# A hybrid decoder block: the next block's x rounded in one run, v ahead of the scores, one masked operand per subtile

## The chip, the cores and the metric

The kernel runs on one core of a Trainium2 chip. The metric is the device time of one execution in microseconds (us). A core has TensorE (PE, matrix products), VectorE (DVE), ScalarE (ACT), GpSimd (POOL) and SyncE (SP, which here only issues DMA transfers). PE writes its results to PSUM, eight banks of 2 KB for each of 128 partitions, and DVE and ACT read them there. Every engine runs its own stream of instructions in order and waits on semaphores.

## What is computed

One layer over 4096 tokens of width 1024: a normalised input, one input projection, three mixers (pooling, convolution, attention in a sliding window), a gate on each, one output projection and a last normalisation. The change touches the attention and what feeds it:

```python
h = rms_norm(x, ln_g[l])
proj = jnp.einsum('bsd,de->bse', h, w_in[l])
(u_pool, g_pool, c_a, c_b, g_conv, q, k, v, g_attn) = split_columns(proj)
...
# attention: 8 query heads on 2 key heads of 64, window of 128 tokens
qb = q.reshape(B, nb, BLOCK, N_KV_HEADS, Q_PER_KV, HEAD_DIM) * (HEAD_DIM ** -0.5)
kb = jnp.concatenate([kr[:, :-1], kr[:, 1:]], axis=2)   # the tile before, and the own
scores = jnp.where(valid, scores + bias, -1e30)         # ALiBi; 0 <= distance < 128
p = jax.nn.softmax(jnp.concatenate([scores, sink], axis=-1), axis=-1)[..., :-1]
out = jnp.einsum('bnkgqs,bnskd->bnqkgd', p.astype(v.dtype), vb)
...
x = x + jnp.einsum('bse,ed->bsd', y, w_out[l])
return rms_norm(x, final_g)
```

## The kernel before

The program has two stages. The attention stage goes through eight blocks of 512 tokens (`NB`), each of four subtiles of 128 (`SUB`). The mixer and output stage behind it starts with `cb0` at line 346's products and is not touched.

Projections are made in fp32 accuracy from three products: weights and x are each split into a rounded part (`hi`, by ACT) and a remainder (`lo`, by DVE), and hi·hi, lo·hi and hi·lo are added up. A tile of the projection (`project`) is 8 slices of x (`kk`) by 3 matmuls of 128x512, so 24. A block has ten tiles in this order: k, q0 to q3, v, g0 to g3. The q tiles fill the four `wide` banks, which later hold the scores; the others take the two `pair` banks in turn. `K_LAG` lets the products with the remainder run three slices behind in k.

x of the next block (n+1) is prepared in block n: loaded into `xs` (two DMAs on SP, two on ACT, `load`), squared and summed (`square` on ACT, lines 239; `square_more` on DVE, line 248), folded on PE (`fold_sums`, line 276, in q3, into bank `turn0`), made a mean (`mean`, DVE, line 282) and a root (`root`, POOL), scaled (`scale`, ACT, line 294, four parts), turned in squares of 32 (`turn_squares`, DVE, line 301), and split (`split_hi`, ACT, line 333; `split_lo`, DVE, line 339) into `xT`, where it overwrites the slices of block n: `spent` says that g3 has used them. `store_xT` sends `xT` to HBM in two pieces of 2 MB for the later stage.

The attention of a subtile j: `scores` on PE (lines 1280, 1289) into `wide`; `take_scores` on DVE in two halves of four heads (mask by `copy_predicated`, line 1037; bias and row maximum, line 1041; then line 1046 and 1047); `exps` on ACT (lines 902, 905); `invert` on DVE; `normalise` on POOL (line 845); `turn_squares_of_probs` on DVE (line 1066), which turns squares of 32 inside the tile `rows`; `store_probs` and `load_probs` on SP, which go through HBM (`p_scratch`) so that the squares come back in transposed places, into `whole`; and `mask` on POOL (lines 855, 856). The window needs two operands: where a query's 64 tokens ("early" or "late" half) see only a part of a key tile, keys of one half belong to the tile before and keys of the other to the own tile. `mask` writes the part for one tile into `rest` (times `rest_mask`) and cuts `whole` down to the other (times `whole_mask`), for each half in turn. `attend` (line 1220) multiplies them with v of the two tiles, for two subtiles at a time (a batch): batch 0 of block n stands behind k of block n+1, batch 1 behind the first scores of block n+1. It writes banks `turn0` and `turn1`; `output` on DVE (line 1201) multiplies by the gate.

Beside this, every block makes up to five combinations of output weights (`Combos`): a sum on DVE (line 488), rounding on ACT (line 496), remainder on DVE (line 500), and a store on SP (line 506), through a buffer `stage` with two places, so that a combination waits for the store of the one two before it. SP's order in a block is: x loads, `load_probs` 2, `store_probs` 3, `load_probs` 3, xT piece 0, combinations 0 and 1, xT piece 1, combinations 2 to 4, `y`, then `store_probs` and `load_probs` 0 and 1, `store_probs` 2.

All orders are written out by hand in the `body` function of each engine. The wait before k is in `by_hi` and `by_lo` (lines 1248 to 1257): each slice of k waits for its own `hi_done` and `lo_done`.

## Time and profile before

| | |
|---|---|
| three runs, median (lowest to highest) | 1538.51 us (1533.78 to 1542.35) |
| the profiled execution | 1539.87 us |
| its span, first to last instruction | 1537.9 us |
| mean granted TensorE clock | 0.947 |
| busy: PE, DVE, ACT, POOL | 90%, 79%, 36%, 33% of the span |
| DMA | 230.78 MB, mean 150 GB/s |

An instruction's row in a timeline has its start and its duration in us, the engine, the line, the operation, output and inputs, and in brackets how long the engine stood idle before it and what released it. "PE" is a matmul, "PEld" a load of weights, "SPq" and "ACTq" the issue of a DMA. The granted clock is a share of full speed: 1.00 is 2.4 GHz, 0.50 is 1.2 GHz. Line numbers are those of the kernel before.

### The profile page before, as it was taken

To read this page: it belongs to the slowest core of one execution; us is meant where nothing else is said; L and a number is where in the kernel's file an instruction comes from. 1 tells how busy PE (TensorE), PEld (TensorE's weight loads), DVE (VectorE), ACT (ScalarE), POOL (GpSimd) and SP (SyncE) were. 2 spreads that over 40 slices of the span, in tenths; PEclk is the share of its full clock that TensorE was granted. 3 is DMA by queue.
4 is the path that set the end of the run, shared out by engine and by line. 5 is a ranking of instruction groups with operands and counts; after the bars stand their busy time and mean duration, and the time that the engine had idled before them with its cause. 6 is when DMAs were issued, how large, how long until landed. Compare 5 with 4: busy or idle time off the path is not lost.

```text
span 1537.9 us, 20630 instructions
## 1 busy us (share of the span) xinstructions
PE 1389.8 (90%) x7070; PEld 1136.8 (74%) x7070; DVE 1210.8 (79%) x2365; ACT 547.1 (36%) x1421; POOL 509.2 (33%) x640
## 2 busy tenths in 40 slices
PE   6978789787887978789599999999999999999998
PEld 5757677575766757577488888888888888888886
DVE  5676766677767666756298999898899998888886
ACT  5644535445444444534022122112113143333332
POOL 4243543435354334545201001001011044555552
PEclk9989989898898989899799999999999999999999
DMA  9636264462726444295623123213143746454442
GB/s 213 198 94 235 83 208 170 125 241 87 251 83 194 163 123 192 81 285 146 166 90 123 41 111 124 79 72 123 47 158 136 280 178 228 165 164 164 165 136 82
DMA packets 112426, 230.78 MB, mean 150 GB/s; under 512 B 16464, under 2 KB 74192, under 8 KB 104656
## 3 DMA queue, kind: packets, MB, share of 16 engines
q1 hardware_dynamic: 88192, 205.85, 38.9%
q10 hardware_dynamic: 24144, 23.80, 6.0%
q8 instruction: 49, 0.80, 0.2%
q14 instruction: 41, 0.34, 0.1%
HBM read 131.05 MB, written 98.57 MB: 149 GB/s over the span
## 4 chain that ended last, share of the span: by engine, by line
PE 46%; DVE 7%; DMA 2%; ACT 1%; SPq 1%; issue 1%; POOL 1%; ACTq 0%; POOLq 0%; DVEq 0%
PE wide L346 11%; PE wide L347 11%; PE wide L348 11%; DVE m_tail L2024 3%; PE turn L346 2%; PE pair L346 2%; PE turn L347 2%; PE pair L347 2%; PE pair L348 2%; PE turn L348 2%; DMA p_scratch<-a_rows 1%; DVE x_first L2121 1%; POOL a_rows L856 1%; PE turn L1220 1%; DVE a_rows L1041 1%
## 5 line engine op out<-in xcount | busy, mean ns | idle before, releaser
L2024 DVE SCALAR_TENSOR_TENSOR m_tail<-m_tail,m_taps 128x512 f32<-128x512 f32 x480 | 338.3, 749 | 4.6
L1251 PE MATMUL pair<-xT,w_hi 128*128 128x512 f32 x384 | 161.7, 421 | 76.0 <-ACT xT L333 72.6
L845 POOL TENSOR_SCALAR a_rows<-a_rows,a_inv 128x128 f32<-128x128 f32 x256 | 102.5, 420 | 225.8 <-DVE a_inv L1061 177.6
L1252 PE MATMUL pair<-xT,w_lo 128*128 128x512 f32 x384 | 157.6, 410 | 0.0
L1766 POOL TENSOR_TENSOR operand_sums<-m_y 128x512 f32<-128x512 f32 x75 | 101.9, 1359 | 167.9 <-PE wide L348 116.7
L1257 PE MATMUL pair<-xT,w_hi 128*128 128x512 f32 x384 | 154.3, 411 | 0.0
L1251 PEld LDWEIGHTS pair<-xT,w_hi 128*128 128x128 f32 x384 | 76.4, 199 | 100.5 <-ACT xT L333 80.0
L108 POOL TENSOR_TENSOR pool_carrier<-pool_carrier 128x1 f32<-128x1 f32 x23 | 14.1, 614 | 395.1 <-DVE m_meanvar L2033 395.1
L346 PE MATMUL wide<-x_first,w_hi 128*128 128x512 f32 x320 | 125.4, 392 | 0.0
L346 PE MATMUL wide<-xT,w_hi 128*128 128x512 f32 x320 | 125.2, 391 | 0.0
L348 PE MATMUL wide<-x_first,w_hi 128*128 128x512 f32 x320 | 124.6, 389 | 0.0
L347 PE MATMUL wide<-x_first,w_lo 128*128 128x512 f32 x320 | 124.5, 389 | 0.0
L348 PE MATMUL wide<-xT,w_hi 128*128 128x512 f32 x320 | 124.5, 389 | 0.0
L347 PE MATMUL wide<-xT,w_lo 128*128 128x512 f32 x320 | 124.5, 389 | 0.0
L1251 PE MATMUL wide<-xT,w_hi 128*128 128x512 f32 x256 | 107.0, 418 | 0.0
L1853 ACT ACTIVATE x_first<-operand_sums 128x512 fp32r<-128x512 f32 x80 | 50.5, 633 | 153.8 <-POOL operand_sums L1766 152.5
L1252 PE MATMUL wide<-xT,w_lo 128*128 128x512 f32 x256 | 104.4, 408 | 0.0
L1257 PE MATMUL wide<-xT,w_hi 128*128 128x512 f32 x256 | 104.2, 407 | 0.0
L905 ACT ACTIVATE a_rows<-a_rows,a_negmax 128x128 f32<-128x128 f32 x256 | 98.7, 387 | 0.0
L1257 PEld LDWEIGHTS pair<-xT,w_hi 128*128 128x128 f32 x384 | 78.2, 204 | 18.0 <-DVE xT L339 0.2
L1252 PEld LDWEIGHTS pair<-xT,w_lo 128*128 128x128 f32 x384 | 76.9, 200 | 14.2
L1086 DVE SCALAR_TENSOR_TENSOR a_q<-wide,a_q 64x512 fp32r<-64x512 f32 x64 | 44.1, 689 | 53.5 <-ACT a_q L894 52.7
(262 smaller groups left out, 3324.6 us busy)
## 6 DMA issues: line engine op xcount, KB each, us to landing
xT_scratch<-xT SPq DMA_DIRECT2D x16, 2048.0 KB, 8.0
p_scratch<-a_rows SPq DMA_DIRECT2D x32, 512.0 KB, 2.6
x_first<-xT_scratch SPq DMA_DIRECT2D x16, 1024.0 KB, 8.2
xT<-xT_scratch SPq DMA_DIRECT2D x16, 1024.0 KB, 9.0
combo_scratch<-stage SPq DMA_DIRECT2D x28, 512.0 KB, 4.4
m_y<-y_scratch ACTq DMA_DIRECT2D x14, 1024.0 KB, 6.7
xs<-in_x_dram SPq DMA_DIRECT2D x20, 512.0 KB, 8.5
a_pT<-p_scratch SPq DMA_DIRECT2D x64, 128.0 KB, 3.9
```

Source lines behind the costliest of these rows:

```text
L346: nc.tensor.matmul(out, w_hi, x_hi, start=first, stop=False)
L347: nc.tensor.matmul(out, w_lo, x_hi, start=False, stop=False)
L348: return nc.tensor.matmul(out, w_hi, x_lo, start=False, stop=last)
L845: last = nc.gpsimd.tensor_scalar(probs[b][:, h], probs[b][:, h], inv[:, b, h:h + 1], 0.5, ALU.mult, ALU.mult)
L905: last = nc.scalar.activation(probs[b][:, h], probs[b][:, h], ACT.Exp, bias=negmax[:, b, h:h + 1], accum_out=rowsum[:, b, h:h + 1])
L1086: last = nc.vector.scalar_tensor_tensor(out=q[halves[1 - kv], head, :], in0=q_bank(t)[halves[odd], :], scalar=HD ** -0.5, in1=q[halves[kv] ...
L1251: nc.tensor.matmul(out, w.hi(c)[:, kk, cols], st.hi[:, kk, :], start=(kk == 0), stop=False)
L1252: nc.tensor.matmul(out, w.lo(c)[:, kk, cols], st.hi[:, kk, :], start=False, stop=False)
L1257: last = nc.tensor.matmul(out, w.hi(c)[:, kk, cols], st.lo[:, kk, :], start=False, stop=(kk == KT - 1))
L1766: nc.gpsimd.tensor_tensor(operand_sums[:, i, 1], y_block(q, left), y_block(q, right), SIGN[op]).then_inc(operand_sum, 1)
L1853: nc.scalar.activation(operands[:, i, 0], operand_source(q, i), ACT.Copy).then_inc(operand_hi, 1)
L2024: nc.vector.scalar_tensor_tensor(out=conv[:, i, :], in0=h[:, i, j:j + TB], scalar=taps[:, i, j:j + 1], in1=conv[:, i, :], op0=ALU.mult, op ...
```

## The change

1. **x of the next block in one run.** ACT splits slices 0 to 6 of x of block n+1 behind the exponentials of subtile 2, then computes the tanh of g3, then slice 7, and only then the exponentials of subtile 3 (`AHEAD` is 7, not 4). DVE makes all eight remainders between the two halves of `take_scores` of subtile 3. Nothing of it stands at the start of the next block any more.
2. **v ahead of the scores.** After q3, PE first attends batch 1 of the block before, with a new wait for DVE's mean (`rstd_steps`), then projects v, then makes the first scores. The scores of subtiles 1, 2 and 3 go into g1, g2 and g3 after slice 1, 2 and 3. The scaling, exponentials, turns and gates on ACT and DVE are put in another order to match; ACT's and DVE's squares move ahead of q1 and write into `tanh` instead of `pT`.
3. **One masked operand.** `store_probs` puts the squares in transposed places as it writes (four DMAs in place of one), so `load_probs` reads whole rows: one DMA into `whole` and two into `rest`, which gets its own copy of the half that it needs (three DMAs in place of four, 768 KB in place of 512). `mask` multiplies `rest` by `rest_mask` over all 128 partitions in one operation; `whole` is not masked. `attend` multiplies `whole` with one tile's v everywhere, and `rest` with `v_step`, the difference between the two tiles' v, which DVE makes once a block in two subtractions.

```diff
@@ store_probs, load_probs
-        need(sp, p_loaded[b], 16 * RUNS * (m // 2))
-        sp.dma_start(p_scratch[b], rows[:, b]).then_inc(p_stored[b], 16)
+        need(sp, p_loaded[b], 16 * LOADED * (m // 2))
+        squares = p_scratch[b].rearrange("(s r) (a e) -> a r s e", r=SQ, a=RUNS)
+        for a in range(RUNS):
+            sp.dma_start(squares[a], rows[a * SQ:(a + 1) * SQ, b].rearrange("r (s e) -> r s e", s=RUNS)).then_inc(p_stored[b], 16)
...
-        squares = p_scratch[b].rearrange("(a r) (s e) -> s r a e", r=SQ, s=RUNS)
-        for s in range(RUNS):
-            sp.dma_start(whole[b][s * SQ:(s + 1) * SQ].rearrange("r (a e) -> r a e", a=RUNS), squares[s]
+        sp.dma_start(whole[b], p_scratch[b]).then_inc(p_loaded[b], 16)
+        for late in range(2):
+            sp.dma_start(rest[b][halves[late]], p_scratch[b][halves[late], late * D // 2:(late + 1) * D // 2]
                          ).then_inc(p_loaded[b], 16)
@@ mask (POOL)
-            for late in range(2):
-                part = runs(whole[b][:, late * D // 2:(late + 1) * D // 2], halves[late])
-                nc.gpsimd.tensor_tensor(runs(rest[b], halves[late]), part, over_heads(rest_mask, halves[late]), ALU.mult)
-                nc.gpsimd.tensor_tensor(part, part, over_heads(whole_mask, halves[late]), ALU.mult).then_inc(masked, 1)
-                pool.wait_ge(masked, 2 * m + late + 1)
+            part = rest[b].rearrange("p (a h c) -> p a h c", a=2, h=HEADS)
+            over_heads = rest_mask.rearrange("p (a c) -> p a c", a=2).unsqueeze(2).to_broadcast([P, 2, HEADS, SQ])
+            nc.gpsimd.tensor_tensor(part, part, over_heads, ALU.mult).then_inc(masked, 1)
@@ vector, body
+            def step_of_v():
+                dve.wait_ge(v_ready, 2 * n + 1)
+                for late, (to, of) in enumerate(((slice(1, 1 + SUB), slice(0, SUB)), (slice(0, SUB), slice(1, 1 + SUB)))):
+                    last = nc.vector.tensor_tensor(v_step[halves[late]], v[halves[late], to], v[halves[late], of], ALU.subtract)
+                last.then_inc(v_ready, 1)
...
                 take_scores(n, 2, 1)
+                step_of_v()
                 inverts(2)
-                next_x(3)
                 gate_make(n, 2)
-                for kk in range(PIECE):
+                take_scores(n, 3, 0)
+                for kk in range(KT):
                     st.split_lo(dve, n + 1, kk)
-                for kv in range(KV):
-                    take_scores(n, 3, kv)
+                take_scores(n, 3, 1)
                 turn_squares_of_probs(SUB * n + 2)
@@ tensor, body
-            pe.wait_ge(q_taken, GROUP * (n + 1))
-            scores(n, 0)
             if not first:
+                if not final:
+                    pe.wait_ge(st.rstd_steps, st.chain(n + 1, 2))
                 attend(pe, n - 1, 1)
-            project(n, "v")
...
             else:
-                project(n, "g0", halfway(lambda: scores(n, 1, lambda: turn_v(n))))
-                project(n, "g1")
-                scores(n, 2)
-                project(n, "g2")
-                project(n, "g3", halfway(lambda: scores(n, 3)))
+                project(n, "v")
+                pe.wait_ge(q_taken, GROUP * (n + 1))
+                scores(n, 0)
+                project(n, "g0")
+                project(n, "g1", after(1, lambda: scores(n, 1, lambda: turn_v(n))))
+                project(n, "g2", after(2, lambda: scores(n, 2)))
+                project(n, "g3", after(3, lambda: scores(n, 3)))
                 project(n + 1, "k")
```

PE in block 1, from the last matmul of q3 on, before: lines 1280 and 1289 are the scores, line 1220 the attend, `pair` the bank of v.

```order
L1257 MATMUL wide<-xT,w_hi 128x512
L1280 MATMUL wide<-a_k_lo,a_q 128x256 x8
L1289 MATMUL wide<-a_k_hi,a_q 128x256 x8
L1220 MATMUL turn<-a_pT,a_v 64x128 x8
L1220 MATMUL turn<-a_rows,a_v 64x128 x8
```

The same place after the change (lines 1294 and 1303 are the scores, 1232 the attend):

```order
L1271 MATMUL wide<-xT,w_hi 128x512
L1232 MATMUL turn<-a_pT,a_v 64x128 x8
L1232 MATMUL turn<-a_rows,a_v 64x128 x8
L1232 MATMUL turn<-a_pT 64x128 x8
L1232 MATMUL turn<-a_rows,a_pT 64x128 x8
L1265 MATMUL pair<-xT,w_hi 128x512
```

The attend has moved ahead of v, the scores behind its 24 matmuls, and the second half of the attend's products has `v_step` (in `a_pT`) in place of v.

ACT at the end of a block before: line 905 is an exponential, 912 the tanh of a gate, 333 the rounding of x, 930 the start of the next block.

```order
L294 ACTIVATE xs<-xs,a_rstd 128x256 x4
L912 ACTIVATE a_tanh<-pair 128x512
L333 ACTIVATE xT<-xs,a_gain 128x512 x4
L902 ACTIVATE a_sinkexp<-a_sinkdiff 128x4
L905 ACTIVATE a_rows,a_rowsum<-a_rows,a_negmax 128x4x32 x4
L912 ACTIVATE a_tanh<-pair 128x512
L902 ACTIVATE a_sinkexp<-a_sinkdiff 128x4
L905 ACTIVATE a_rows,a_rowsum<-a_rows,a_negmax 128x4x32 x4
L333 ACTIVATE xT<-xs,a_gain 128x512 x4
L189 DMA xs<-in_x_dram 32x16x256 x2
L930 ACTIVATE a_k_hi<-a_k_hi 128x2x128
```

And after:

```order
L333 ACTIVATE xT<-xs,a_gain 128x512 x7
L906 ACTIVATE a_tanh<-pair 128x512
L333 ACTIVATE xT<-xs,a_gain 128x512
L896 ACTIVATE a_sinkexp<-a_sinkdiff 128x4
L899 ACTIVATE a_rows,a_rowsum<-a_rows,a_negmax 128x4x32 x4
L896 ACTIVATE a_sinkexp<-a_sinkdiff 128x4
L899 ACTIVATE a_rows,a_rowsum<-a_rows,a_negmax 128x4x32 x4
L189 DMA xs<-in_x_dram 32x16x256 x2
L924 ACTIVATE a_k_hi<-a_k_hi 128x2x128
```

The second four slices have moved from behind the last exponentials to ahead of them.

SP between two blocks before: line 690 is `store_probs`, 699 `load_probs`, 733 the first piece of xT.

```order
L690 DMA p_scratch<-a_rows 128x1024
L189 DMA xs<-in_x_dram 32x16x256 x2
L699 DMA a_pT<-p_scratch 32x4x256 x4
L690 DMA p_scratch<-a_rows 128x1024
L699 DMA a_rows<-p_scratch 32x4x256 x4
L733 DMA xT_scratch<-xT 128x4096
L506 DMA combo_scratch<-stage 128x2x512
```

And after:

```order
L695 DMA p_scratch<-a_rows 32x4x256 x4
L189 DMA xs<-in_x_dram 32x16x256 x2
L702 DMA a_pT<-p_scratch 128x1024
L704 DMA a_pT<-p_scratch 64x512 x2
L695 DMA p_scratch<-a_rows 32x4x256 x4
L702 DMA a_rows<-p_scratch 128x1024
L704 DMA a_rows<-p_scratch 64x512 x2
L730 DMA xT_scratch<-xT 128x4096
L506 DMA combo_scratch<-stage 128x2x512
```

The order is the same; a store has four issues in place of one, a load three in place of four.

## Rows read from the trace of the kernel before

**Rows 1.** Busy time by stretches: from:to, then busy (instructions) of PE, PEld, DVE, ACT, POOL

```profile
108.97:653.87 544.90, 453.51 (x2630) 363.38 (x2632) 383.13 (x984) 253.11 (x820) 232.16 (x294) 0.88 0.47 161
185.80:199.20 13.40, 4.92 (x12) 3.86 (x13) 11.15 (x34) 6.31 (x23) 5.93 (x9) 0.50 0.12 47
...
223.30:230.00 6.70, 6.19 (x16) 4.96 (x17) 4.59 (x11) 2.44 (x4) 0.47 (x1) 0.50 0.44 131
```

**Rows 2.** Who waited for whom, TensorE's waits: us in total, times, longest

```profile
PE pair L1251 <- ACT xT L333: 72.6, 7, 10.5
...
PE turn L1220 <- POOL a_rows L856: 19.1, 2, 16.5
PE wide L1280 <- DVE a_q L1086: 18.7, 8, 3.8
...
PE turn L276 <- DVE a_sumsq L248: 16.3, 6, 3.2
```

**Rows 3.** Timeline of TensorE in block 2, from the k tile to g0

```profile
194.28 0.79 PE L1251 MATMUL pair<-xT,w_hi 128*128 128x512 f32 x1 [10.54 <-ACT xT L333]
...
200.26 1.09 PE L1220 MATMUL turn<-a_pT,a_v 128*64 128x128 f32 x16
...
203.19 0.50 PE L1251 MATMUL wide<-xT,w_hi 128*128 128x512 f32 x1
...
223.81 0.58 PE L276 MATMUL turn<-a_sumsq,a_fold 128*128 128x16 f32 x2 [2.61 <-DVE a_sumsq L248]
...
239.63 0.50 PE L1251 MATMUL pair<-xT,w_hi 128*128 128x512 f32 x1
...
248.03 0.74 PE L1280 MATMUL wide<-a_k_lo,a_q 64*128 64x256 f32 x8
```

**Rows 4.** Timeline of DVE in block 2

```profile
203.32 1.39 DVE L1077 TENSOR_TENSOR a_k_lo<-pair,a_k_hi 64x512 fp32r<-64x512 f32 x2 [2.66 <-ACT a_k_hi L934]
...
205.95 1.23 DVE L1066 STREAM_TRANSPOSE a_rows<-a_rows 128x1024 f32<-128x1024 f32 x1
...
218.28 1.50 DVE L248 CUSTOM_DVE_ANT_0 a_pT<-xs 128x256 f32<-128x256 f32 x1
...
223.24 0.41 DVE L248 CUSTOM_DVE_ANT_0 a_pT<-xs 128x256 f32<-128x256 f32 x1
...
238.98 0.70 DVE L1037 COPY_PREDICATED wide<-a_rows,wide 128x512 f32<-128x512 uint32 x1
...
241.07 0.69 DVE L1037 COPY_PREDICATED wide<-a_rows,wide 128x512 f32<-128x512 uint32 x1
...
272.64 6.46 DVE L339 SCALAR_TENSOR_TENSOR xT<-xs,a_gain,xT 128x512 fp32r<-128x512 f32 x4 [0.27 <-ACT xT L333]
...
285.71 3.04 DVE L339 SCALAR_TENSOR_TENSOR xT<-xs,a_gain,xT 128x512 fp32r<-128x512 f32 x4 [0.19 <-ACT xT L333]
```

**Rows 5.** The page's fifth part, the exponentials on ACT: busy, mean ns of one

```profile
L905 ACT ACTIVATE a_rows<-a_rows,a_negmax 128x128 f32<-128x128 f32 x256 | 98.7, 387 | 0.0
```

**Rows 6.** DMA landings: combination store of block 2; x loads; stores of probabilities

```profile
combo_scratch<-stage SPq DMA_DIRECT2D x1, 512.0 KB, 8.3
...
DMA to landing us min/median/max: 6.4/10.1/15.7
...
DMA to landing us min/median/max: 2.6/2.6/10.2
```

**Rows 7.** Timeline of ACT in block 2, behind q3

```profile
237.59 0.63 ACT L496 ACTIVATE stage<-raw 128x512 fp32r<-128x512 f32 x1 [2.84 <-DMA combo_scratch<-stage]
238.13 1.69 ACT L294 ACTIVATE xs<-xs,a_rstd 128x256 f32<-128x256 f32 x4
```

**Rows 8.** Timeline of POOL: a scaling in block 2, and masks of the last subtile

```profile
269.43 1.41 POOL L845 TENSOR_SCALAR a_rows<-a_rows,a_inv 128x128 f32<-128x128 f32 x4 [0.42 <-DVE a_inv L1061]
...
748.78 1.25 POOL L855 TENSOR_TENSOR a_rows<-a_rows 64x512 f32<-64x512 f32 x1 [0.99 <-DMA a_rows<-p_scratch]
```

More of the change, by code:

```diff
@@ L944, in body @@
                 w.split_hi(act, CHUNK_Q + 1)
+            if not first and not final:
+                act.wait_ge(free(slot("g3")), earlier(n - 1, slot("g3")) + 1)
+                st.square(act, n + 1)
             q_hi(n, 1)
-            if not first and not final:
-                st.square(act, n + 1)
             for s in combos.of_block(n, (1,)):
@@ L1119, in body @@
             make_combos(n, (0,))
+            if not first and not final:
+                st.square_more(dve, n + 1)
             for t in range(1, GROUP):
@@ L1128, in body @@
                 make_q_lo(n, t)
-                if t == 1 and not first and not final:
-                    st.square_more(dve, n + 1)
                 make_combos(n, (t,) if t < 3 else (3, 4))
@@ L1230, in attend @@
                     for odd in range(2):
-                        last = product(s, late, kv, odd, 1 - late, halves[late], False, s == 1 and kv == 1)
+                        last = product(rest[s], v_step[:, 2 * batch + s], 0, s, late, kv, odd, halves[late], False,
+                                       s == 1 and kv == 1)
         last.then_inc(pv_full, 1)
```

162 lines of the change are left out of this document (87 added, 75 removed).

## The prediction

> **What bounds the kernel now.** I read the share of busy time first, then the granted clock by stretches, then who waited for whom, then one block's timeline on each engine. TensorE is busy 90% of the span, so the time is its work, its idle time and its slow time. The eight blocks of 512 tokens of the attention stage take half of the span, and from one k tile's end to the next, six times, they take 544.90 us, 90.8 us a block, at a mean clock of 0.88 [rows 1]. The mixer and output stages behind them run at full clock without a gap worth naming, and the change leaves them alone.
>
> In the list of waits TensorE's longest is before the k tile, for ACT's rounding of x: 72.6 us, 7 times; then the fold of the sums of squares, 16.3 us in 6, and the first scores, 18.7 us in 8 [rows 2]. In block 2 the first two are idle times of 10.54 and 2.61 us [rows 3], and the scores wait 2.3 on the mean of the eight. Each brings half clock (1.2 of 2.4 GHz): around the k wait 13.4 us of it, of which TensorE worked 4.9, and after the fold 6.7 us [rows 1]. Such work takes twice as long, so a block loses about 2.5 us behind the first wait and about 5 behind the other two. 90.8 is then near 15 of idle, 7 of slow clock and 69 of work. The work checks: 36 matmuls in 8.4 us [rows 3] make 5.6 for a tile of 24, ten tiles 56; two attends of 2.93 (200.26 to 203.19); four scores of about 1.9; the fold.
>
> Why does k wait? The second half of x's tiles is rounded behind the last exponentials, and those wait for DVE, which first has four remainders to make. With the masks on POOL beside them these take 6.46 us, without them 3.04 [rows 4].
>
> **The change part by part.** I walk one steady block of the changed kernel, 0 being the end of k on TensorE; durations are those of block 2.
>
> *Start of the block.* DVE now makes all eight remainders between the two halves of the last scores, and k ends some 0.3 behind the eighth. DVE then takes the second half, 2.1 (238.98 to 241.07 [rows 4]); ACT's four exponentials are 4 x 0.387 + 0.2 = 1.75 [rows 5]; its two x loads take 0.9 to issue, and k's own split takes ACT 3.0 (k ended by 200.3, DVE took over at 203.32 [rows 3, 4]), then DVE 1.39. With the product with the gate, 1.3, and the turn of the last probabilities, 1.24, DVE reaches q0's remainder at 11.4. TensorE has done attend and q0 by 8.5, so 2.9 of this stands on the path.
>
> *Up to the mean.* On DVE: q0 1.4; a combination 2.1 (sum, ACT's rounding, remainder); eight squares, 0.41 each free, 1.5 beside a mask [rows 4], so 3.3 to 5; q1, a combination, q2: at 26. The third combination needs the stage buffer of the first. Its store stands on SP behind the last probabilities: turned at 11.4, now four store issues of 0.43 where one was, 2.6 to land, three load issues where four were, then the xT store: issued at 17.8. Behind a 2 MB xT store it takes 8.3 to land [rows 6]: 26.1. That meets DVE there, and the mean is made at 28.4. TensorE has attended (2.9), done q0 to q3 (22.4) and folded (0.4): 25.7. The squares are ahead of the fold by about 5 us, so its wait goes. In its place stands the new wait for the mean ahead of the second attend (the fold's result lies in attend's bank): 28.4 - 25.7 = 2.7 us, where the fold and the scores had 4.7. Queued behind it are attend, v and the scores, all needed by DVE.
>
> *From the mean to k.* Attend 2.9, v 5.6, 1.4 to the first half of the scores: 38.3. v ahead of the scores hides the wait for the last q remainder, at no cost while that is under 8.5 (it was 2.3). But the softmax starts one v later. From there a chain leads through DVE and ACT: second scores 8.5 later (TensorE's spacing, 239.63 to 248.03); two takes and a turn 5.4; inverses, x's third turn, exponentials 2.3; tanh and gate 1.2; the fourth scaling, 1.69 [rows 7], less 0.4 of overlap, and its turn 1.2; two takes and a turn 5.4; the step of v, two 64-row subtractions, 1.3 (as k's remainder, 1.39); 1.6 for exponentials, inverses and gate; a take 2.1; eight remainders at 0.76, 6.1. Sum 36.4. Two masks of subtiles 0 and 1 fall there. Before, four masks lengthened four remainders by 3.4 [rows 4]; two give about 0.8 here, as one of them runs beside the take. Bounds: 0 and 3.4.
>
> By that chain k ends at 38.3 + 36.4 + 0.8 + 0.3 = 75.8. The wait for the mean, 2.7, is as long as the fold's, which brought 6.7 us of half clock [rows 1, 3], and the work behind it is on the chain; 3.4 to 6.7 us of half clock cost 1.7 to 3.3. I take 2.2: **78 us a block**, 12.8 less. Of k's wait about 3 us stays, spread between its matmuls, as they follow the remainders.
>
> The Trainium skill (SBUF — State Buffer, "SBUF: two separate sides") says that a POOL operation and a DVE operation with two SBUF inputs hold a shared port exclusively, so that the other fully blocks. The trace has DVE at half pace, not stopped: 6.46 for four. By the rule two masks of 1.3 could block 2.6 us of the remainders instead of 0.8, and the block would be 79.8 and the time 1451.
>
> *Masks.* One operation over 128 partitions by 512 columns in place of four over 64 by 512, each 1.25. No row shows the new shape; four scalings of 128 by 128 take 1.41 together [rows 8], which speaks for columns, not partitions, so I take 1.3 (bounds 1.3, and 2.6 if partitions counted). It saves 3.7 a subtile, off TensorE's path but for the end. Loads carry 256 KB more for a subtile, 1 MB a block: at the stage's 161 GB/s [rows 1] 6.5 us of transfers, hidden where the DMA share is 0.47; if that cover went, they would fall on the stage buffer's wait. TensorE has the same matmuls as before; the operand v_step changes none.
>
> *The single blocks.* Block 0 loses its k wait and half clock, 10.4 + 2.5, and a little at the scores: 13.5. The last block loses the waits for q (2.3), for masks (19.1 - 16.5 = 2.6) and some 1.2 of its 1.4 before the last scores: 6.1. At the very end TensorE stands 16.5 us for the last masks [rows 2]; four masks of 1.25 from 748.78 on [rows 8], 5.0, become 1.3, three more store issues cost 1.3, one load issue fewer gives 0.4: 2.9 less.
>
> Sum: 6 x 12.8 + 13.5 + 6.1 + 2.9 = 99.3. The profiled execution took 1539.9 (span 1537.9), 1.4 above the median; **1440 us**.
>
> **The rivals.** *All waits hide.* If the combinations and x arrive early, the mean is ready before q3 ends and the clock stays up: 69.6 of work, 1.2 before the last scores and 1.2 in k give 72; six blocks save 112.9, the time is 1404. For: two store issues more is all that SP gets there. Against: in block 2 a combination already waited 2.84 us on ACT for its buffer [rows 7].
>
> *DVE's chain grows.* A block shrinks by a seventh and DMA carries more, so x (6.4 to 15.7 us to land, median 10.1 [rows 6]) and the stage buffer come late, each us of it on the mean; with the masks at 3.4, x's and the buffer's landings 2 longer and both at half clock 6.7, a block is 84: 22.5 + 6 x 6.8 = 63, 1476. In this class also falls that the k wait is only moved: DVE starts the first remainder only after the last scores, four tiles into g3, and if these came 6 us later the same 84 would result. For: DVE has no slack in the loop. Against: a DMA share of 0.47 [rows 1] has room for a seventh more.
>
> *Slower.* The probabilities of the last subtile, x and the combinations go through SP's single queue in series ahead of the mean. At the longest landings (store 10.2, x 15.7 [rows 6], and xT taken like x) the first combination's store is issued at about 26 and lands at 42, the mean is at 44, and the fifth combination waits once more, so that the first scores are taken at 59, not 38: 99 a block, 6 x 8.2 = 49 lost against 22.5 gained, **1566**. It decides from 94.6 a block on. For: such a landing stands in the trace. Against: the median store lands in 2.6; the 10.2 is from the last block with 3 MB of weights ahead.
>
> **How the numbers follow.** The forecast has 0.58, its own range 1425 to 1462 (period 76 to 81); all waits hidden 0.12; the grown chain 0.26; slower 0.03; 0.01 for no change. The range 1412 to 1480 leaves out the first rival's core, the tail of the second, and the slower one. Half a percent, 8 us, is what a measurement can tell from no change: faster 0.95, same 0.02, slower 0.03.
>
> **What would show it.** k ends about every 78 us; TensorE's wait for ACT's rounding before k is under 2 us; the fold waits for nothing; a new wait of 2 to 5 us for DVE's mean stands before the attend that follows q3, with half clock behind it; eight remainders in one run of 6.1 to 7.5; the last wait near 13.6. Wrong if that attend waits for masks instead (SP's chain), if the fold waits for x, or if DVE's run of remainders takes 9 or more.

## The result and the profile after

The changed kernel takes **1485.7 us** (median of 4 runs, 1484.0 to 1488.9) against 1540.4 of the kernel before (4 runs): a ratio of 0.965, 95% interval 0.962 to 0.969. The forecast was 1440, 1412 to 1480. The direction was right, the time was not: 54.7 us were gained where 100 were expected. The profiled execution has a span of 1482.0 us, beside 1537.9 before. TensorE's busy share in the page's first part, busy us (share of the span) xinstructions:

```profile
PE 1368.3 (92%) x7070; PEld 1118.1 (75%) x7070; DVE 1174.0 (79%) x2381; ACT 548.4 (37%) x1421; POOL 362.0 (24%) x543
```

POOL's time is 362 us of the span where it was 509, and TensorE is busy 92% where it was 90%.

The first view is the busy time by stretches; its columns are from:to, length, then busy (instructions) of PE, PEld, DVE, ACT and POOL, granted clock, DMA share, GB/s. The stretch is the one from block 0's k tile to block 6's, as in [rows 1].

```profile
93.54:592.49 498.95, 434.14 (x2631) 346.81 (x2632) 349.13 (x997) 253.77 (x820) 119.04 (x222) 0.95 0.60 188
```

498.95 us for six blocks are **83.16 us a block**; before it was 90.8, and the forecast was 78. The mean clock rose from 0.88 to 0.95. In this stretch POOL's busy time fell from 232 to 119 us, and the rate of transfers rose from 161 to 188 GB/s.

The second view is TensorE's list of waits (us in total, times, longest); it answers to [rows 2].

```profile
PE turn L1232 <- DVE a_meansq L282: 50.6, 6, 11.1
PE turn L1232 <- POOL a_rows L850: 24.6, 2, 17.8
PE pair L1271 <- DVE xT L339: 10.4, 28, 0.7
...
PE turn L276 <- DVE a_sumsq L248: 0.9, 2, 0.8
```

The three waits of before are gone: of the 72.6 us ahead of k, 10.4 in small pieces are left, the fold waits 0.9 in all, the scores for q not at all. In their place stands one new wait, for DVE's a_meansq ahead of the second attend: 50.6 us in six, a mean of 8.4, where 2.7 was forecast. The waits for masks grew from 19.1 to 24.6.

Block 2 shows the new wait on TensorE (start, us, then the instruction; idle time before it and its releaser in brackets), and the k tile's end ahead of it:

```profile
174.99 0.49 PE L1271 MATMUL pair<-xT,w_hi 128*128 128x512 f32 x1 [0.16 <-DVE xT L339]
175.41 1.09 PE L1232 MATMUL turn<-a_pT,a_v 128*64 128x128 f32 x16
...
208.66 1.97 PE L1232 MATMUL turn<-a_pT,a_v 128*64 128x128 f32 x16 [7.63 <-DVE a_meansq L282]
```

k ends at 175.5 without a wait worth naming; 25.5 us later TensorE has nothing to do, stands 7.63 us and comes back at half clock: the same 16 matmuls take 1.97 us where they took 1.09 at 175.41.

DVE in the same block tells why:

```profile
168.53 6.41 DVE L339 SCALAR_TENSOR_TENSOR xT<-xs,a_gain,xT 128x512 fp32r<-128x512 f32 x8
...
192.37 0.42 DVE L248 CUSTOM_DVE_ANT_0 a_tanh<-xs 128x256 f32<-128x256 f32 x1 [4.69 <-issue]
...
194.80 1.51 DVE L248 CUSTOM_DVE_ANT_0 a_tanh<-xs 128x256 f32<-128x256 f32 x1
...
206.32 0.69 DVE L488 TENSOR_TENSOR stage_sum<-raw 128x512 f32<-128x512 f32 x1 [5.02 <-DMA combo_scratch<-stage]
...
208.43 0.17 DVE L282 TENSOR_SCALAR a_meansq<-turn 128x16 f32<-128x16 f32 x1
```

The eight remainders run without a break in 6.41 us. But the squares start only at 192.37, when x has landed (ACT's square at 192.40 names that transfer), and the third combination stands 5.02 us for the store that frees its stage buffer. The mean, queued behind it, is made at 208.43, which is 32.9 us behind k; the forecast had 28.4.

SyncE's queue (the issues, with the time that issuing took) and the landings of two tensors in this block:

```profile
178.20 2.23 SPq L695 DMA_DIRECT2D p_scratch<-a_rows  x4
180.48 1.50 SPq L189 DMA_DIRECT2D xs<-in_x_dram  x2
186.39 0.34 SPq L702 DMA_DIRECT2D a_pT<-p_scratch  x1
...
187.96 2.00 SPq L695 DMA_DIRECT2D p_scratch<-a_rows  x4
195.53 0.34 SPq L702 DMA_DIRECT2D a_rows<-p_scratch  x1
...
197.18 0.45 SPq L730 DMA_DIRECT2D xT_scratch<-xT  x1
197.68 2.60 SPq L506 DMA_DIRECT2D combo_scratch<-stage  x2
```

```profile
DMA to landing us min/median/max: 8.2/8.3/8.5
...
DMA to landing us min/median/max: 3.5/6.0/7.2
```

The first of the two lines is the combinations' stores, the second the stores and loads of probabilities. What the stage buffer waits for is not only a slow landing. The probabilities of subtile 2 are now turned behind the run of remainders, so their store is issued 2.7 us behind k's end, where in block 2 of the kernel before it was issued 7.3 us ahead of it (192.99, with k ended at 200.3). Both of the last two subtiles now go through this queue behind k. Each load has to wait for its store to land: the load at 186.39 waits for the store of 178.20 and holds up the next store, whose rows DVE had turned at 185.5; the load at 195.53 waits for that one. So the combination's store is issued at 197.7, 22.2 us behind k (forecast 17.8), and lands 8.6 us later behind xT's 2 MB (forecast 8.3).

### The profile page after: what moved, and what is told of

It reads as the page before. It is cut to its first block, busy times and chain, and to the rows that moved or that the text cites. A ratio compares the mean times of both kernels' runs of the same rounds, so it can differ in the third digit from the quotient of the medians.

```text
span 1482.0 us, 20609 instructions
## 1 busy us (share of the span) xinstructions
PE 1368.3 (92%) x7070; PEld 1118.1 (75%) x7070; DVE 1174.0 (79%) x2381; ACT 548.4 (37%) x1421; POOL 362.0 (24%) x543
## 4 chain that ended last, share of the span: by engine, by line
PE 57%; DVE 19%; DMA 12%; SPq 5%; ACT 4%; issue 3%; POOL 1%; POOLq 0%; DVEq 0%; ACTq 0%
PE wide L346 12%; PE wide L347 12%; PE wide L348 12%; DMA p_scratch<-a_rows 6%; DVE a_rows L1043 4%; DMA combo_scratch<-stage 3%; DVE m_tail L2042 3%; PE turn L1232 3%; DVE xT L339 3%; DVE wide L1039 2%; PE pair L1265 2%; DVE a_rows L1068 2%; PE pair L1266 2%; PE pair L1271 2%; ACT a_rows L899 2%
## 5 line engine op out<-in xcount | busy, mean ns | idle before, releaser
L1271 PE MATMUL pair<-xT,w_hi 128*128 128x512 f32 x384 | 154.2, 401 | 11.0 <-DVE xT L339 10.4
L840 POOL TENSOR_SCALAR a_rows<-a_rows,a_inv 128x128 f32<-128x128 f32 x256 | 94.3, 388 | 282.0 <-DVE a_inv L1063 223.7
L1265 PE MATMUL pair<-xT,w_hi 128*128 128x512 f32 x384 | 151.6, 395 | 3.5 <-DVE w_lo L410 3.5
L1266 PE MATMUL pair<-xT,w_lo 128*128 128x512 f32 x384 | 150.5, 392 | 0.0
L346 PE MATMUL wide<-xT,w_hi 128*128 128x512 f32 x320 | 125.2, 391 | 0.0
L348 PE MATMUL wide<-xT,w_hi 128*128 128x512 f32 x320 | 124.5, 389 | 0.0
L347 PE MATMUL wide<-xT,w_lo 128*128 128x512 f32 x320 | 124.5, 389 | 0.0
L1271 PEld LDWEIGHTS pair<-xT,w_hi 128*128 128x128 f32 x384 | 72.2, 188 | 39.6 <-DVE xT L339 24.3
L1265 PE MATMUL wide<-xT,w_hi 128*128 128x512 f32 x256 | 101.3, 396 | 0.0
L1271 PE MATMUL wide<-xT,w_hi 128*128 128x512 f32 x256 | 99.8, 390 | 0.0
L1266 PE MATMUL wide<-xT,w_lo 128*128 128x512 f32 x256 | 99.7, 389 | 0.0
L1232 PE MATMUL turn<-a_pT,a_v 128*64 128x128 f32 x256 | 24.6, 353 | 75.1 <-DVE a_meansq L282 50.6
L1265 PEld LDWEIGHTS pair<-xT,w_hi 128*128 128x128 f32 x384 | 72.5, 189 | 17.7 <-DVE w_lo L410 3.9
L1266 PEld LDWEIGHTS pair<-xT,w_lo 128*128 128x128 f32 x384 | 72.4, 189 | 13.9
```

Of the source, the lines that this page charges most:

```text
L346: nc.tensor.matmul(out, w_hi, x_hi, start=first, stop=False)
L347: nc.tensor.matmul(out, w_lo, x_hi, start=False, stop=False)
L348: return nc.tensor.matmul(out, w_hi, x_lo, start=False, stop=last)
L840: last = nc.gpsimd.tensor_scalar(probs[b][:, h], probs[b][:, h], inv[:, b, h:h + 1], 0.5, ALU.mult, ALU.mult)
L1232: return nc.tensor.matmul(out, weights[keys, halves[kv]], probs_of, start=start, stop=stop)
L1265: nc.tensor.matmul(out, w.hi(c)[:, kk, cols], st.hi[:, kk, :], start=(kk == 0), stop=False)
```

## The experiments

Thirteen kernels, all with the kernel before run beside them on the same chip. The chips differ a little: the median of the kernel before lies between 1538.3 and 1542.3 us, so between two kernels a difference of 2 or 3 us can't be told from none. A block's length is read as above, from one attend after k to the next; "the mean's wait" is the line `<- DVE a_meansq` in TensorE's list.

The change has three parts: (1) the next x squared, scaled and rounded in one run behind the last gate, (2) v ahead of the scores, (3) one masked operand, the step between v's tiles, and the stores and loads that go with it.

**e1, part 3 alone.** The order of before, with part 3's masks, stores, loads and step of v. The squares go to the tanh tiles, as in the changed kernel, since v_step takes their place, and ACT's squares wait for g3 to be read.

```
-            for late in range(2):
-                part = runs(whole[b][:, late * D // 2:(late + 1) * D // 2], halves[late])
...
+            nc.gpsimd.tensor_tensor(part, part, over_heads, ALU.mult).then_inc(masked, 1)
...
+                act.wait_ge(free(slot("g3")), earlier(n - 1, slot("g3")) + 1)
...
+                step_of_v()
...
-            pe.wait_ge(v_ready, n + 1)
+            pe.wait_ge(v_ready, 2 * n + 2)
...
-        pe.wait_ge(masked, 2 * subtiles)
+        pe.wait_ge(masked, subtiles)
```

> Part 3 alone on the order of before: stores of four DMAs, loads of three, one mask per subtile, v_step; k still waits for ACT's second four slices. Theory A (the gain of the whole change is the k wait, and what it fell short by is the chain SP, DMA, stage buffer, mean): the four remainders of x beside the masks take 3.1 to 4 us where they took 6.5, so the k wait shrinks from 10.4 to about 8, six or seven times, and the masks' waits in the last block go: 1520 to 1530. Rival R (the new store layout itself makes landings late, all over): the first masks come later than before, and the time is 1540 or more.

Measured: **1479.8 us**, ratio 0.959 (0.957 to 0.962): both expectations were far off. Part 3 alone gains 61 us against the kernel before, more than the whole change. TensorE's waits in it:

```profile
PE pair L1253 <- ACT xT L333: 52.3, 7, 7.6
PE wide L1282 <- DVE a_q L1079: 22.5, 8, 4.8
PE turn L1220 <- POOL a_rows L849: 12.5, 1, 12.5
```

Its block is 83.0 us long. The k wait fell from 10.4 to 7.5 us, as the remainders have fewer masks beside them (900 ns each on average, 1249 before), and the fold's wait is gone, which I had not connected with the masks at all.

**e2, parts 1 and 2 without 3.** The changed kernel with the masks, stores and loads of before.

```
-            nc.gpsimd.tensor_tensor(part, part, over_heads, ALU.mult).then_inc(masked, 1)
+            for late in range(2):
+                part = runs(whole[b][:, late * D // 2:(late + 1) * D // 2], halves[late])
+                nc.gpsimd.tensor_tensor(runs(rest[b], halves[late]), part, over_heads(rest_mask, halves[late]), ALU.mult)
+                nc.gpsimd.tensor_tensor(part, part, over_heads(whole_mask, halves[late]), ALU.mult).then_inc(masked, 1)
...
-                step_of_v()
```

> Parts 1 and 2 without part 3: before's one store, four loads, four masks, no v_step. Theory A: the wait for the mean stays at about 8 us a block, since it hangs on x's landing and on the stage buffer behind the xT store, and the eight remainders grow by 2 to 4 us from the masks beside them: 1495 to 1510. Rival R (the four-part stores delay SP's chain): the wait for the mean falls to 4 or less and the time to 1465 to 1475.

Measured: **1525.3 us**, ratio 0.989 (0.987 to 0.992), worse than either theory said. The wait for the mean is there (32.4 us in six), so it isn't part 3's. And k now waits for seven of its eight remainders, by 0.7 to 1.2 us each, since these run beside a mask. So parts 1 and 2 gain 15 us alone, part 3 gains 61 alone, and together they gain 55: they don't add up.

**e7, the masks' time put back.** Is it the time of the masks on POOL that part 3 saves, or TensorE's and the transfers' new shape? Part 3 alone, each mask done four times (the mask is 0 or 1, so the operand is the same).

```
+            for again in range(3):
+                nc.gpsimd.tensor_tensor(part, part, over_heads, ALU.mult).then_inc(seen_ready, 1)
+                pool.wait_ge(seen_ready, 4 + 3 * m + again + 1)
             nc.gpsimd.tensor_tensor(part, part, over_heads, ALU.mult).then_inc(masked, 1)
```

> Part 3 alone, with the mask on GpSimd done four times over (the operand is 0 or 1, so the result is the same), so that its time for each subtile is what it was in the kernel before (four operations of 1.25 us, now four of 1.29). It asks how much of the 62 us of part 3 is the masks' time on GpSimd, which stands beside DVE's squares and remainders, and how much is the work taken from TensorE and the loads in another form. Theory A (the masks beside DVE's work are what cost): squares take 1.5 us again where a mask runs, the fold wait comes back by 2 to 3 us and the remainders run slower; 30 to 50 us of the gain go, 1510 to 1530 us. Rival R (TensorE's shorter work and the loads are the gain; GpSimd has room): 1480 to 1490 us.

Measured: **1527.4 us** (10 runs), ratio 0.993 (0.990 to 0.995): 48 of the 61 us are gone again. The waits for ACT's rounding and for the squares' sum are back (the first two lines below: TensorE's waits). The next pair is the squares on DVE, the masks once and four times (busy us, mean ns):

```profile
PE pair L1256 <- ACT xT L333: 64.6, 9, 9.6
...
PE turn L276 <- DVE a_sumsq L248: 18.8, 6, 3.7
```

```profile
L248 DVE CUSTOM_DVE_ANT_0 a_tanh<-xs 128x256 f32<-128x256 f32 x48 | 22.5, 533 | 0.2
```

```profile
L248 DVE CUSTOM_DVE_ANT_0 a_tanh<-xs 128x256 f32<-128x256 f32 x48 | 46.2, 1022 | 0.2
```

Of e1 first, then of e7. A square takes 1022 ns on average with the long masks and 533 with the short ones. So the masks' time beside DVE's work is what cost, as theory A has it: what stands on POOL lengthens what DVE does at the same time, and in the order of before that was the fold and k. By blocks, from the attends behind k (107.41 to 635.44 in e7), a block is 88.0 us with the long masks, 83.0 in e1 and 90.8 before the change. So 5.0 of the 7.8 us that part 3 gains in a block are the masks' time; what makes the other 2.8 wasn't tried. The two profiled executions are 40.6 us apart, 30 of it in these six blocks; 9 fall in the last block and the tail, where TensorE waits for the masks themselves (20.0 us in all, 12.5 in e1).

**e3, x's load ahead.** SyncE's two loads of the next x ahead of the third subtile's store.

```
             else:
-                st.load(sp, n + 1, (0, 1))
                 load_probs(sp, n - 1, 2)
...
+            if n < NB - 2:
+                st.load(sp, n + 2, (0, 1))
             store_probs(sp, n, 2)
```

> The changed kernel with SP's two x loads of a block issued ahead of the store of subtile 2's probabilities instead of behind it (some 4 to 5 us earlier). Theory A: squares start 3 to 5 us earlier, the last subtile's store meets an emptier queue and lands in 3 instead of 5.8, the xT store and the first combination's store go out 3 us earlier, the wait for the mean falls by about 3 a block: 1465 to 1472. Rival D (the wait for the mean is DVE's own work and its contention with POOL): no change beyond 3 us, 1483 to 1488.

Measured: **1480.0 us**, 5.7 less than the changed kernel, between the expectations. The waits for x fell (ACT's and DVE's together from 44.6 to 7.3 us), but DVE's and ACT's waits for the stage buffer grew from 32.5 and 24.5 us to 40.3 and 27.4, and the mean's wait stayed at 47.8: x was not what came last.

**e4, xT's stores behind the combinations'.**

```
-            store_xT(n, 0)
-            for s in combos.of_block(n, (0, 1)):
-                combos.store(sp, s)
-            store_xT(n, 1)
-            for s in combos.of_block(n, (2, 3, 4)):
+            for s in combos.of_block(n, range(5)):
                 combos.store(sp, s)
+            for piece in range(PIECES):
+                store_xT(n, piece)
```

> The changed kernel with both 2 MB xT stores of a block issued behind the combinations' stores instead of between them. Theory A: a combination's store lands in 3 to 4.5 us instead of 7 to 10, DVE's wait for the stage buffer ahead of the mean and ACT's behind it go (5.0 and 6.3 in block 2), the wait for the mean falls from 8 to 3 or 4, the block from 83.2 to 77 to 79: 1455 to 1462. Rival D: 1483 to 1488. Against A would also be a gain under 10, if the xT stores, now later, hold up the stores and loads of the next probabilities.

Measured: **1450.5 us**, ratio 0.941 (0.938 to 0.944). 35 us for the order of these stores, a bit more than the 24 to 31 expected. The combinations' stores, their waiters and their landing, in the changed kernel and then in this one:

```profile
  DVE stage_sum L488: 32.5, 6
  ACT stage L496: 24.5, 4
...
DMA to landing us min/median/max: 2.8/7.3/10.2
```

```profile
  DVE stage_sum L488: 8.0, 5
  ACT stage L496: 6.3, 4
...
DMA to landing us min/median/max: 2.7/3.6/6.0
```

TensorE's wait for the mean falls from 50.6 to 20.6 us, 3.4 a block, and in three of the six blocks TensorE comes back at full clock, as here in block 2 (in a fourth the 16 matmuls take 1.20 us):

```profile
168.94 1.09 PE L1230 MATMUL turn<-a_pT,a_v 128*64 128x128 f32 x16
...
197.47 1.09 PE L1230 MATMUL turn<-a_pT,a_v 128*64 128x128 f32 x16 [2.68 <-DVE a_meansq L282]
```

Its second attends stand from 121.65 to 590.19, six blocks of **78.1 us**, with a wait of 2.3 to 5.4 us (77.9 from the attends behind k). That is the length that the forecast had; it needed a stage buffer that comes in time. The terms don't all agree, though: the wait is 0.7 longer than forecast, and half clock, for which 2.2 were forecast in every block, stands behind two of the six waits (and in part behind a third).

**e5, e9 and e11, the same edit without part 1 and 2, without part 3, and on the kernel before.** The diff is e4's.

> Part 3 alone (as in the earlier run, 1479.8 us) with both stores of xT issued behind the five combinations' stores. With the whole change this edit was worth 35 us (1485.7 to 1450.5), because the wait for a_meansq before the first attend fell from a mean of 8.4 us to 3.4. Theory A (parts 1 and 2 pay once the stage buffer is no longer late): with part 3 alone TensorE still waits 7.5 us for k and 2.1 to 4.8 us before the scores, DVE finishes the remainders one by one, so an earlier combination meets work that is late anyway; I expect 1465 to 1477 us, 15 to 27 above the whole change with the same edit. Rival R (parts 1 and 2 are worth nothing or less in any setting): the edit gives its 29 to 35 us here too, 1445 to 1451 us, no slower than 1450.5.

> Parts 1 and 2 without part 3 (1525.3 us), with xT's stores behind the combinations' stores. There the wait for the mean was 4.8 to 7.2 us a block and the eight remainders went one by one beside two masks' work. Theory A (the late stage buffer took parts 1 and 2's gain, masks or not): the wait for the mean falls by 3 to 5 us a block, 1495 to 1507 us. Rival R (with the old masks TensorE waits for the remainders and for squares as long, and an earlier mean only lengthens these waits): 1518 to 1526 us.

> The kernel before with only xT's stores behind the combinations' stores. It asks whether the order of the queue was worth anything before the change, that is whether the change made the stage buffer late or uncovered it. Theory A (uncovered: before, 10.4 us of wait for k and the wait for the squares' sum covered it): no difference, 1530 to 1543 us. Rival R (it was on the path all along): 1500 to 1520 us.

Measured: **1474.6**, **1512.7** and **1540.7 us** (e11: ratio 1.000, 0.998 to 1.002). e5 and e11 fell as theory A had them. e9 lies between: the wait for the mean went nearly (7.9 us in two blocks), but 12.6 us is less than A's 18 to 30. What has taken the rest is in TensorE's and DVE's rows of e9:

```profile
PE turn L1233 <- POOL a_rows L857: 44.2, 7, 19.7
PE pair L1270 <- DVE xT L339: 40.5, 49, 1.2
```

```profile
L339 DVE SCALAR_TENSOR_TENSOR xT<-xs,a_gain,xT 128x512 fp32r<-128x512 f32 x52 | 74.8, 1505 | 0.0
```

A remainder takes 1505 ns there (868 in the changed kernel), and attend waits for the masks themselves. With these runs the table is complete:

| | xT's store ahead | xT's store behind | edit gives |
|---|---|---|---|
| kernel before | 1540.4 | 1540.7 (e11) | 0 |
| part 3 | 1479.8 (e1) | 1474.6 (e5) | 5 (1 by the ratios, 0.959 and 0.958) |
| parts 1, 2 | 1525.3 (e2) | 1512.7 (e9) | 13 |
| the whole change | 1485.7 | 1450.5 (e4) | 35 |

It reads by rows and by columns. Before the change the queue's order was worth nothing, for two reasons. The buffer was hardly late: DVE and ACT waited 8.2 and 2.8 us for it in all blocks, where the changed kernel has 32.5 and 24.5. And what lateness there was stood behind other waits: e11 takes DVE's down to 1.3 and ACT's away, and TensorE's wait for k stays (73.2 us, 72.6 before). So the change both made the buffer late and took away what covered it; how the 35 us divide between the two wasn't tried. By columns: with the store behind, parts 1 and 2 bring 24 us on top of part 3 (1474.6 to 1450.5), with it ahead they cost about 6.

**e6, both orders; e10, the mean ahead as well.** e6 is e3 and e4 together. e10 adds one move on DVE.

```
-                if t == 3 and not final:
-                    st.mean(dve, n + 1)
                 make_q_lo(n, t)
+                if t == 2 and not final:
+                    st.mean(dve, n + 1)
                 make_combos(n, (t,) if t < 3 else (3, 4))
```

> The changed kernel with both orders of the DMA queue moved: the load of the next x ahead of the third subtile's probs store, and xT's stores behind the combinations' stores. Apart they gave 5.7 and 35.2 us. If each takes its own piece off the same chain (x's landing, then the stage buffer), the sum is 41 us: 1445 us; since the second left 3.4 us of wait for the mean and 20 us in six blocks of waits for x, it could be more: 1432 to 1446 us, a period of 75.5 to 77.5. Rival: x's landing is hidden once xT's stores are gone from the front, and the 78.1 us of a block are then work, not waits: 1448 to 1453 us.

> The 1440.6 us kernel (next x's load ahead, xT's stores behind) with DVE's a_meansq made in the turn of q's third tile, ahead of the sum for the third combination, instead of behind it: the mean then no longer stands behind the wait for the stage buffer (15.3 us in six blocks on DVE, 4.2 at most). TensorE's wait for it was 17.8 us in six blocks. Theory A (the last stage wait is all that is late there): that wait falls to under 1 us a block, 2 to 3 us a block less: 1423 to 1430 us. Rival R (the third combination is then late by what the mean gained, and the first take of scores behind it starts no earlier, so attend ends early and the scores wait): 1437 to 1443 us.

Measured: **1440.6 us** (ratio 0.936, 0.931 to 0.941) and **1422.5 us** (0.923, 0.920 to 0.926). The first lies in the range expected. The two orders add up: 5.7 and 35.2 us alone, 45.1 together, and by the ratios 0.005 and 0.024 alone, 0.029 together. e10 fell a little below theory A. What is left of the wait, in block 2 of e10 and in its list:

```profile
190.96 1.09 PE L1231 MATMUL turn<-a_pT,a_v 128*64 128x128 f32 x16 [0.40 <-POOL a_rows L849]
```

```profile
PE turn L1231 <- POOL a_rows L849: 28.0, 7, 18.2
```

From the first attend behind block 0's k, 92.70, to the one behind block 6's, 531.20, its blocks take 73.1 us: the rival in which all waits hide had 72. The stage buffer is still late there (DVE 13.8 us, ACT 7.4), but the mean no longer stands behind it.

**e8, the last block's probabilities ahead of the weights.** On e4.

```
         sp.wait_ge(st.lo_done, KT * NB)
-        for c in (CHUNK_CB, CHUNK_CA, CHUNK_GP):
-            w.load(sp, c, (0, 1))
         load_probs(sp, NB - 2, 2)
...
         load_probs(sp, NB - 2, 3)
+        for c in (CHUNK_CB, CHUNK_CA, CHUNK_GP):
+            w.load(sp, c, (0, 1))
```

> The changed kernel with xT's stores behind the combinations' (1450.5 us) and in addition, ahead of the last block, the probs loads of subtiles 2 and 3 ahead of the six weight loads on the DMA queue. In the changed kernel the attend of the last block waited 6.8 us for masks whose loads landed behind the weights. Theory A: that wait goes and the last weights (needed later) come no later than wanted: 5 to 7 us less, 1443 to 1446 us. Rival R: the last block's projections then wait for the weights by as much, or the wait for the mean stands behind it: 1448 to 1453 us.

Measured: **1449.8 us**, no difference from 1450.5 that can be told. The wait for masks went (17.5 us in one, the tail's, is left), and 5.0 us of a wait for a_q ahead of the last block's scores stand in its place:

```profile
PE turn L1230 <- POOL a_rows L848: 17.5, 1, 17.5
...
PE wide L1292 <- DVE a_q L1086: 5.0, 1, 5.0
```

**e12 and e13, the last probabilities ahead of the next stage's constants.** e12 on e10, e13 on the changed kernel.

```
         sp.wait_ge(score_taken, ATTENDED)
+        w.load(sp, CHUNK_U)
+        attention.turn_loads(sp)
         with nc.allow_non_contiguous_dma(reason="per-channel constants, once"):
...
-        w.load(sp, CHUNK_U)
-        attention.turn_loads(sp)
         w.load(sp, CHUNK_GC)
```

> The 1422.5 us kernel with the loads of the last probabilities, and the store between them, issued ahead of the nine small loads of the next stage's constants on the DMA queue (before and after the change they stand behind them: 607.24 to 617.33, 10 us of issues, then the four of the U weights, which stay in front here). TensorE's last wait for masks was 18.2 us. Theory A (the queue's order sets the last wait, not the masks' time): the first of these loads is issued some 10 us sooner, and the last wait falls to 7 to 10 us: 1411 to 1415 us. Rival R (the store between them waits for DVE's turn and lands no sooner, or the constants come late for the mixer): 1419 to 1424 us.

> The same edit on the changed kernel alone (1485.7 us, last wait for masks 17.8 us, where 13.6 was forecast). Theory A: last wait 7 to 10 us, 1474 to 1479 us. Rival R: 1482 to 1487 us.

Measured: **1414.3 us** (ratio 0.917, 0.913 to 0.920) and **1477.1 us** (0.958, 0.954 to 0.962): 8.2 and 8.6 less, theory A both times. The best kernel of the study is e12, 8.3% below the kernel before. In the changed kernel the last wait was 17.80 us; its SyncE rows show what the loads stood behind (first and last of nine constants, the U weights, then the load):

```profile
668.85 0.46 SPq L1618 DMA_DIRECT2D m_taps<-in_conv_dw_dram  x1
...
678.51 0.44 SPq L1621 DMA_DIRECT2D m_pw<-in_conv_pw_dram  x1
678.99 1.95 SPq L390 DMA_DIRECT2D m_y<-in_w_in_dram  x4
681.03 0.40 SPq L702 DMA_DIRECT2D a_pT<-p_scratch  x1
```

With the loads ahead the wait for masks at the end is 8.4 us in both kernels, in e13:

```profile
PE turn L1232 <- POOL a_rows L850: 15.2, 2, 8.4
```

## Why the prediction was wrong, step by step

**What bounds the kernel.** Right: the k wait, the fold and the half clock behind each were on the path, and a kernel without them takes 73.1 us a block (e10). What the reading missed is why the fold waited. [rows 4] had a square at 1.50 and one at 0.41 us, and I used them only as a spread for one step. The masks stood beside the squares before the change too, so part 3 removes that wait by itself (e1), and most of part 3's worth in a block is the masks' time (e7).

**Start of the block.** Right in time: the eight remainders took 6.41 us (forecast 6.1, and 0.8 for two masks), though by two errors that offset each other (see the masks below). q0's remainder came 10.1 us behind k (forecast 11.4), and what was left of k's wait is 1.5 us a block (forecast about 3). The mask of 128 by 512 took 1.29 us (forecast 1.3) where nothing held it up.

**Up to the mean: this step failed.** Three terms of it were too small, all on SyncE's queue. The probabilities' store was taken at 2.6 us to land, the median of [rows 6], but it lands while x's 2 MB are under way, and takes 5.6 to 6.0; and the store and load of the subtile before, which the sum left out, hold the queue for 2.4 us more. So the queue came out at 17.8 us where 22.2 was measured, though DVE had the rows turned 1.4 us sooner than forecast. x itself landed 16.9 us behind k; I had its squares begin without a wait, and they waited 4.69, though that was hidden in block 2: DVE was done with q2's remainder at 201.3 and then stood 5.02 for the buffer all the same. And what was taken as one wait for the stage buffer came twice: the fifth combination stands again (DVE 6.25 us in block 2), and the way from the mean to the first take became 13.1 where 9.9 and 2.2 of slow clock were forecast (the slow attend takes 4.55 us, the one at full clock 2.94, so the clock cost 1.6). The mean at 32.9 instead of 28.4 makes the wait 7.6 in block 2 and 8.4 on average, 5.7 more than forecast; the block is 5.2 longer. e3 and e4 tell the terms apart: x's load is worth 1 us a block, xT's place ahead of the combination 5.1 (83.2 to 78.1). The 8.3 us that the combination's store takes I had read from the trace and put into the sum, without asking what stands ahead of it; e4 is that question, and gives back a block of the forecast's length.

**From the mean to k.** Right in sum: 35.6 us from the first take to the last remainder in block 2, where 36.4 and 0.8 were forecast. DVE's chain didn't grow, and the remainders' wait is 0.7 at most. v ahead of the scores hid the wait for q.

**The masks beside DVE: misread, and covered by luck.** The prediction read the four remainders of 6.46 us as DVE at half pace, not stopped. The rows of the changed kernel around block 2 show a stop. Here are three masks on POOL, each followed by the operation of DVE that met it:

```profile
167.22 1.29 POOL L850 TENSOR_TENSOR a_pT<-a_pT,a_rows 128x512 f32<-128x512 f32 x1
167.27 1.27 DVE L1048 TENSOR_SCALAR a_negmax<-a_rowmax 128x4 f32<-128x4 f32 x1
...
168.97 1.45 POOL L850 TENSOR_TENSOR a_rows<-a_rows 128x512 f32<-128x512 f32 x1 [0.46 <-DMA a_rows<-p_scratch]
...
169.19 1.77 DVE L339 SCALAR_TENSOR_TENSOR xT<-xs,a_gain,xT 128x512 fp32r<-128x512 f32 x1
...
194.59 1.44 POOL L850 TENSOR_TENSOR a_pT<-a_pT,a_rows 128x512 f32<-128x512 f32 x1 [12.52 <-DMA a_pT<-p_scratch]
...
194.80 1.51 DVE L248 CUSTOM_DVE_ANT_0 a_tanh<-xs 128x256 f32<-128x256 f32 x1
```

An operation on 4 columns takes 0.17 us elsewhere and 1.27 here, and ends 0.03 behind the mask's end; the remainder ends 0.55 behind it and the square 0.28. In the kernel before, all 28 remainders that start during a mask end 0.55 us behind the mask's end. A mask in turn lasts up to 1.73 us where a remainder is still running as it starts, so the two engines take turns: four masks met four remainders one by one, and that is the 6.46. Operations that read PSUM, and the turns, run through: a turn at 263.84 took its 1.23 us under a mask of the kernel before, and q1's remainder at 215.07 its 0.68. The Trainium skill (SBUF — State Buffer, "SBUF: two separate sides") says that one engine holds the port exclusively and the other is fully blocked, and these rows agree with it. For the block at hand the two masks cost DVE 1.1 and 1.0 us, 2.1 in all, where the sum has 0.8 and the rule 2.6. That the chain came out right is luck: a free remainder takes 0.74 us and the next starts 0.66 behind it, so eight take 5.4 where 6.1 was put. With 2.6 the block would have been 79.8 and not 78; what makes it 83.2 is the stage buffer, and with that in time (e4) it is 78.1.

**Single blocks.** Block 0 lost 15.4 us (forecast 13.5): k ends at 93.54, before at 108.97. The last block lost nothing, it took 2.1 more where 6.1 less was forecast: attend waits 6.77 us for masks whose loads landed behind the weights (TensorE, then POOL):

```profile
624.18 1.98 PE L1232 MATMUL turn<-a_pT,a_v 128*64 128x128 f32 x16 [6.77 <-POOL a_rows L850]
```

```profile
621.19 2.84 POOL L850 TENSOR_TENSOR a_rows<-a_rows 128x512 f32<-128x512 f32 x1 [5.95 <-DMA a_rows<-p_scratch]
```

The forecast had the 2.6 us of before go with the masks' time. Before the change they were the masks' time: the load had landed at 676.2, 22.3 us behind k's end, and the four masks ran until 685.4. Now there is one mask, but the load lands 28.7 us behind k's end, and that is what the forecast left out. e8 shows that this wait covers another of 5 us, for q. The tail took 3.1 more instead of 2.9 less. The masks did fall, but a subtile's load is issued behind nine constants, so its end is fixed by that queue, and TensorE, which now gets there earlier, waits longer. e13 gives 8.6 us by the order alone. In e1 the last wait was 12.5: TensorE comes to the end of g3 5.0 us later there (669.12 against 664.13), and that load is issued 2.3 us sooner (678.76 against 681.03).

The sum of the measured terms: 15.4 + 6 x 7.66 - 2.1 - 3.1 = 56.2, the difference of the spans 55.9. The forecast's 99.3 is 43 more: 31 from the blocks, 8 from the last block, 6 from the tail, less 2 from block 0. With the blocks' error alone the time would have been 1471, inside the range; the single blocks, each read from one row and without the queue behind it, put it outside.

**The rivals.** "DVE's chain grows" gave 84 a block and 1476; it named the stage buffer and x, which is what came late, but priced with masks at 3.4 us and half clock as well. It was nearest to the time, for two of its three reasons; that 84 stands so close to 83.2 is in part luck, as the masks cost 2.1 and not 3.4. "All waits hide" at 72 a block was right about the work: e10 has 73.1. Of its condition, that combinations and x arrive early, the forecast rightly said that block 2 spoke against it.

## What to carry to other kernels

A wait on the busiest engine covers the lateness of other things, and moving work to take the wait away can make them later still, so before pricing its removal, write down for each transfer when it will now be issued, when it lands and who is next to wait for it; the order of xT's store was worth 0 us before this change and 35 after it. A landing time isn't a property of the transfer: take it with what will be in flight then, and ask of every large one in the queue whether the small one that someone waits for could go first. Work on an engine with time to spare isn't free where it runs beside another engine's; repeating it with the same result, as e7 does, prices it in one run.

## What the runs showed of the hardware that was not expected

An operation of DVE that starts while POOL runs a mask ends a fixed time behind the mask's end: 0.03 us for one on 4 columns, 0.28 for a square, 0.55 for a remainder. So it lasts as long as the mask still has to run, and not a fixed share longer: a square of 128 by 256 took 1.51 us instead of 0.42, a remainder up to 1.77 instead of 0.74, the mean of 48 squares went from 533 to 1022 ns when each mask was done four times. Operations that read PSUM, and the turns, took their usual time. A POOL operation over 64 partitions by 512 columns took 1.25 us and one over 128 by 512 took 1.29, so here twice the partitions cost 0.04. The 512 KB stores of the combinations, with 2 MB stores issued ahead of them on the same queue, landed after a median of 7.3 us over the stage, and after 3.6 with the 2 MB behind them (e4). An attend behind a wait of 2.68 us (e4) or 3.35 us (e9) ran at full clock, 1.09 us for 16 matmuls, and one behind 4.06 us (e4) or 7.63 us (the changed kernel) at half, 1.97; one behind 3.42 us in e9 ran at half too.
